# Earlier row loads, pool sums by thirds and DMA transposes in a streaming encoder layer on eight cores

## The reference

```
xn = rmsnorm(x); u, B, C, h = split(xn @ w_in)            # 4 x 512 columns
pool: per group of 128 channels, window w = 2, 4, 8, 16:
      mean of u over the last w rows - u, times w_pool[g], scaled
conv: B * (causal width-3 convolution of C * h)
x += rmsnorm(concat(group_rmsnorm(pool), group_rmsnorm(conv)) @ w_out)
x += rmsnorm(cross_attention(rmsnorm(x), memory keys and values))
x += rmsnorm(square(relu(rmsnorm(x) @ w_up)) @ w_down)
```

## Time and profile before

| what | us |
|---|---|
| median of 3 runs | 898.96 (898.18 to 900.38) |
| profiled execution, its own time | 901.45 |
| its span (core 1, the slowest) | 900.1 |
| spans of the eight cores | 893.8 to 900.1 |
| TensorE busy on core 1 | 859.5 (95%) |
| DVE busy, ACT busy | 448.9 (50%), 432.4 (48%) |

### The profile page before, as it was taken

How to read it: one execution, slowest core, us unless ns; L and a number is a source line. 1 busy time by engine, 2 the same in 40 slices (tenths; PEclk the granted TensorE clock), 3 DMA queues, 4 the chain that set the end, 5 groups by cost and what they waited for, 6 DMA issues and landing times.

```text
span 900.1 us, 14693 instructions; the slowest of 8 cores (893.8 to 900.1 us)
## 1 busy us (share of the span) xinstructions
PE 859.5 (95%) x5018; PEld 453.0 (50%) x5018; DVE 448.9 (50%) x772; ACT 432.4 (48%) x1043; POOL 53.0 (6%) x66
## 2 busy tenths in 40 slices
PE   7898898999999999999999998999899999999996
PEld 4565444664456666544444443457454444444442
DVE  3788687476872222232142877886684222200133
ACT  4557888466873333332132386886684333200122
POOL 1100100000000000000001000000000000000000
PEclk9989989999999999999999999999999999999998
DMA  9997376719585654636829992171716746426022
GB/s 195 194 155 110 76 118 105 127 28 206 76 151 81 98 80 62 102 88 115 117 100 120 236 228 82 40 96 23 95 21 110 107 69 94 59 36 87 8 94 94
DMA packets 66793, 91.89 MB, mean 102 GB/s; under 512 B 2936, under 2 KB 58360, under 8 KB 66208
## 3 DMA queue, kind: packets, MB, share of 16 engines
q0 software_dynamic: 58080, 60.95, 48.1%
q1 hardware_dynamic: 8640, 30.00, 10.2%
HBM read 137.49 MB, written 12.30 MB: 166 GB/s over the span
## 4 chain that ended last, share of the span: by engine, by line
PE 80%; ACT 9%; issue 4%; DVE 4%; DMA 2%; ACTq 0%; DVEq 0%; SPq 0%; POOLq 0%
PE psum L393 77%; PE psum L397 3%; ACT stg L411 3%; ACT xsb L411 3%; ACT st L411 2%; ACT un L411 2%; DMA ring<-w_in 1%; DMA X<-xp 1%; DVE un L423 1%; DVE xT L414 1%; DMA conv_p<-stg 1%; DVE X L423 0%; DVE un L414 0%; DVE un L418 0%; DVE xsb L418 0%
## 5 line engine op out<-in xcount | busy, mean ns | idle before, releaser
L393 PE MATMUL psum<-xT,ring 128*128 128x352 bf16 (+6 forms) x2336 | 413.0, 333 | 3.6 <-DVE xT L414 2.5
L393 PEld LDWEIGHTS psum<-xT,ring 128*128 128x128 bf16 x2336 | 226.5, 98 | 167.5 <-issue 6.6
L393 PE MATMUL psum<-ring,un 128*128 128x512 bf16 (+1 forms) x1408 | 302.6, 380 | 0.0
L411 ACT ACTIVATE un<-psum 128x352 bf16<-128x352 f32 (+9 forms) x258 | 125.0, 492 | 201.2 <-PE psum L393 198.9
L393 PEld LDWEIGHTS psum<-ring,un 128*128 128x128 bf16 (+1 forms) x1408 | 130.7, 98 | 157.7 <-issue 9.1
L414 DVE TENSOR_TENSOR un<-un 128x352 bf16<-128x352 bf16 (+5 forms) x176 | 84.8, 483 | 156.8 <-ACT un L411 156.8
L414 DVE TENSOR_TENSOR stg<-psum,gp 128x1024 f32<-128x1024 f32 (+3 forms) x51 | 53.1, 1042 | 106.6 <-ACT stg L411 57.6
L411 ACT ACTIVATE stg<-psum 128x1024 bf16<-128x1024 f32 (+3 forms) x51 | 44.5, 873 | 104.8 <-PE psum L393 102.6
L414 DVE TENSOR_TENSOR xT<-psum,gcs 128x1024 bf16<-128x1024 bf16 (+2 forms) x52 | 60.0, 1155 | 35.7 <-PE psum L397 35.2
L393 PE MATMUL psum<-ring,mg 128*128 128x512 bf16 (+1 forms) x320 | 75.8, 388 | 0.0
L423 DVE SCALAR_TENSOR_TENSOR X<-stg,st,X 128x1024 f32<-128x1024 f32 (+3 forms) x51 | 56.3, 1104 | 6.8 <-DVE stg L414 4.7
(11 more groups left out here) (95 smaller groups left out, 517.1 us busy)
## 6 DMA issues: line engine op xcount, KB each, us to landing
ring<-w_up POOLq DMA_DIRECT2D x16, 1024.0 KB, 14.2
ring<-w_down POOLq DMA_DIRECT2D x16, 1024.0 KB, 10.7
X<-xp SPq DMA_DIRECT2D x16, 512.0 KB, 14.0
yp<-X SPq DMA_DIRECT2D x16, 512.0 KB, 2.7
ring<-w_in POOLq DMA_DIRECT2D x7, 1024.0 KB, 11.4
ring<-w_out POOLq DMA_DIRECT2D x4, 1024.0 KB, 31.8
ring<-w_q POOLq DMA_DIRECT2D x4, 1024.0 KB, 22.7
stg<-xp SPq DMA_DIRECT2D x8, 512.0 KB, 4.3
```

The costliest lines, as they stand in the source:

```text
L393: P.add("pe", lambda e: e.matmul(out, lhsT=lhsT, rhs=rhs, start=start, stop=stop), reads=[lhsT, rhs], writes=[out])
L411: P.add("act", lambda e: e.activation(out=out, in_=in_, func=func, scale=scale, **kw), reads=rd, writes=wr)
```

## The change

- SP's queue loses the identity and the gain columns (`idf`, `gcs`), which ACT's queue asks for now. Block 2's load (L1181) waits for block 1 to have landed, not for w_in.
- The chain that makes blocks ready is written anew. Block 2 (number 3) is prepared wholly ahead of the first projection; block 3 (number 4) behind the second unit; fewer fillers. It uses five bf16 slots in another place, for which the pool scratch `SW` shrinks.
- Pool sums go in three tiles of columns (272, 512 and 288 with the running streams) and the first enters at unit 4 of phase 0, among the preparation of blocks 4 to 7.
- Mappings of the first tile begin at (1, 3) and not (1, 8); those of the last end at (3, 1) and not (3, 4).
- The evacuations of u that DVE does are units 4 to 7 and not 5, 7, 9, 11. The adds that fill `psel` go to the end of phase 3.
- In `hook0`, the 8 TensorE transposes per block of group 1 become one DMA transpose on SP's queue, and the gain is multiplied in place 7 units later.

```diff
--- before.py
+++ after.py
@@ -281,9 +281,9 @@
 
 U_TILES = [[(0, 272), (272, 528), (528, 784), (784, 1072)], [(16, 528), (528, 1040)]]
 A_TILES = [[(14, 368), (368, 720), (720, 1072)], [(16, 528), (528, 1040)]]
-P_TILES = [[(0, 528), (528, 1072)], [(16, 528), (528, 1040)]]
-P_AT = [(12, 16), (4, 8)]
-MAP_AT = [[[(1, 8), (1, 9), (1, 10), (1, 11)], [(2, 3), (2, 5), (2, 7), (2, 9)], [(2, 11), (3, 0), (3, 2), (3, 4)]],
+P_TILES = [[(0, 272), (272, 784), (784, 1072)], [(16, 528), (528, 1040)]]
+P_AT = [(4, 12, 16), (4, 8)]
+MAP_AT = [[[(1, 3), (1, 5), (1, 7), (1, 9)], [(1, 11), (2, 1), (2, 3), (2, 5)], [(2, 7), (2, 9), (2, 11), (3, 1)]],
           [[(1, 4), (1, 5), (1, 6), (1, 7)], [(2, 2), (2, 3), (2, 4), (2, 5)]]]
 F_TILES = [[(16, 368), (368, 720), (720, 1072)], [(16, 528), (528, 1040)]]
 Q_TILES = [F_TILES[0], [(16, 400), (400, 784), (784, 1040)]]
@@ -593,7 +593,7 @@
     V_OFF = 4 * UW * 4
     P_OFF = V_OFF + 4 * VW * 4
     S_OFF = P_OFF + 4 * MW * 2
-    SW = [592, 528]
+    SW = [528, 528]
     sA_OFF = S_OFF
     sB_OFF = [sA_OFF + 16 * w for w in SW]
     SQ_OFF = [sB_OFF[g] + 12 * SW[g] for g in range(2)]
@@ -782,7 +782,7 @@
                     k = P_AT[grp].index(n_all)
                     poolq.extend((P_TILES[grp][k][0], f) for f in pool_ops(grp, *P_TILES[grp][k]))
                 if ph == 0:
-                    ev_u(jj, proj(w, jj, lo, hi), lo, hi, grp == 0 and n in (5, 7, 9, 11))
+                    ev_u(jj, proj(w, jj, lo, hi), lo, hi, grp == 0 and 4 <= n < 8)
                 elif ph == 1:
                     ev_C(jj, proj(w, jj, lo, hi), lo, hi)
                 elif ph == 2:
@@ -1168,17 +1168,17 @@
 
     halo = stg[0:16, 0:D]
     memx = [uf(PT_OFF + 8192, 1024), uf(PT_OFF + 12288, 1024)]
-    xs_pro = [ub(P_OFF + 2048 * i, 1024) for i in range(4)]
+    xs_pro = [ub(V_OFF + 2048 * i, 1024) for i in range(5)]
     xs_mem = [ub(KVP_OFF + 2048 * i, 1024) for i in range(2)]
     stT = mgf[0:32, 0:512]
     scT = mgf[0:4, 512:1024]
     dma("sp", halo, xh[:, :], rd=False)
     first = stream.load_first()
     dma("sp", Xs(0), xrow(0, 0), rd=False)
-    dma("sp", idf[:, :], ident[:, :], rd=False)
-    dma("sp", gcs[:, :], gcol[:, :], rd=False)
+    dma("act", idf[:, :], ident[:, :], rd=False)
+    dma("act", gcs[:, :], gcol[:, :], rd=False)
     dma("sp", Xs(1), xrow(0, 1), rd=False)
-    P.add("sp", lambda e: e.dma_start(out=Xs(2), in_=xrow(0, 2)), reads=[first], writes=[Xs(2)], dma=True)
+    P.add("sp", lambda e: e.dma_start(out=Xs(2), in_=xrow(0, 2)), reads=[Xs(1)], writes=[Xs(2)], dma=True)
     for b in (3, 4):
         dma("sp", Xs(b), xrow(0, b), rd=False)
     dma("sp", pvt[:, :], pvec[:, :], rd=False)
@@ -1192,7 +1192,7 @@
     stream.load(after=Xs(4))
     vmemset(epsb[:, :], EPS)
     vmemset(ones[:, :], 1.0)
-    vmemset(ub(S_OFF, 512), 1.0)
+    vmemset(ub(65536, 512), 1.0)
     vmemset(bd64[:, :], 0.0)
     vmemset(bd64[0:64, 0:64], 1.0)
     vmemset(bd64[64:128, 64:128], 1.0)
@@ -1201,14 +1201,10 @@
         dma("sp", stT[b * 16 + 1:b * 16 + 16, :], spool[b], rd=False)
     dma("sp", scT, sconv.rearrange("b r c -> (b r) c"), rd=False)
     vcopy(idb[:, :], idf[:, :])
-    tt(psel[:, 0:32], idf[:, 0:32], idf[:, 32:64], ALU.add)
-    tt(psel[:, 0:32], psel[:, 0:32], idf[:, 64:96], ALU.add)
-    tt(psel[:, 0:32], psel[:, 0:32], idf[:, 96:128], ALU.add)
-
     pre_q = [(halo, 16, 9, 0, xT3[:, :, 0:16])]
     for b in (0, 1, 2, 3, 4, 5, 6, 7, SMP):
         pre_q.append((Xs(b), rows(b), skey(b), 0, xT3[:, :, xcol(b):xcol(b) + rows(b)]))
-    pre_xs = [xs_pro[k % 4][0:q[1], :] for k, q in enumerate(pre_q)]
+    pre_xs = [xs_pro[k % 5][0:q[1], :] for k, q in enumerate(pre_q)]
 
     pre_tb = {}
 
@@ -1228,7 +1224,7 @@
         xap, r, key, gi, dst = pre_q[k]
         gain_out(pre_tb.pop(k), r, gi, dst)
 
-    warm = ub(S_OFF, 512)
+    warm = ub(65536, 512)
 
     def c_w(n):
         out = bank()
@@ -1239,9 +1235,9 @@
         for w in text.split():
             {"A": c_a, "S": c_s, "T": c_t, "G": c_g, "W": c_w}[w[0]](int(w[1:]))
 
-    CHAIN = {0: "A3", 2: "A4", 3: "W8 S3 T3 G3 W8 S4 T4 G4 A5 A6 W4", 4: "A7", 5: "S5 T5 S6 G5 A8", 6: "T6 G6", 7: "S7 A9",
-             8: "T7 S8 G7", 9: "T8 G8", 10: "S9", 11: "W3 T9 G9 W2"}
-    chain("W11 A0 A1 S0 T0 G0 W2 A2 S1 T1 G1 W7 S2 T2 G2 W5")
+    CHAIN = {0: "A4", 1: "S4 T4 G4", 2: "A5", 3: "A6", 4: "A7", 6: "S5 W2 T5", 7: "S6 W3 G5 T6 W3 G6 A8",
+             8: "S7 T7 A9", 9: "G7 S8", 10: "T8 G8 S9", 11: "W2 T9 G9 W2"}
+    chain("W11 A0 A1 S0 T0 G0 W2 A2 S1 T1 S2 G1 W3 T2 G2 A3 W6 S3 T3 G3")
 
     def states_in():
         tb = tbank()[0]
@@ -1258,6 +1254,10 @@
                 states_in()
             elif n == 15:
                 tt(psg[:, :], pvt[:, 0:4], pvt[:, 16:20], ALU.mult)
+        elif phase == 3 and n == 11:
+            tt(psel[:, 0:32], idf[:, 0:32], idf[:, 32:64], ALU.add)
+            tt(psel[:, 0:32], psel[:, 0:32], idf[:, 64:96], ALU.add)
+            tt(psel[:, 0:32], psel[:, 0:32], idf[:, 96:128], ALU.add)
         elif phase == 2 and n == 0:
             load_gp("g_mix_post")
 
@@ -1287,7 +1287,9 @@
             xs = pre_a(sl, 128, 12 + j % 2)
             if j + 2 < NB:
                 dma("sp", sl, xrow(1, j + 2), rd=False)
-            later(2, lambda: pre_b(xs, 128, 0, xT3[:, :, xcol(j):xcol(j) + 128]))
+            dst = xT3[:, :, xcol(j):xcol(j) + 128]
+            P.add("sp", lambda e: e.dma_start(out=dst, in_=xs, transpose=True), reads=[xs], writes=[dst], dma=True)
+            later(7, lambda: tt(dst, dst, gcs[:, 0:8].unsqueeze(2).to_broadcast([128, 8, 128]), ALU.mult))
 
     def cache_loads():
         for mc in range(2):
```

## The result

The changed kernel takes **905.45 us** (4 executions, 905.04 to 905.64) against 898.57 of the kernel before beside it on the chip: ratio 1.0073, 95% interval 1.0056 to 1.0091. It is slower by 6.9 us, where 2.8 less was forecast, and lies above the range. The profiled execution's own time is 905.28; its slowest core is 7.

A forecast was written before the change was run, and what follows sets the result against it. TensorE was taken to wait for VectorE in phase 0 and VectorE and ScalarE in phase 3, and to be bound by its own work under w_down; 5.0 - 4.2 - 3.6 = -2.8, from 898.96 to 896.2 us, range 891 to 903.

The forecast's parts named there:

- Step 1: First loads: block 2 lands at 16, w_in at 18.5, so the first projection starts at about 19.7, 3.2 us later.
- Step 2: Block 3's preparation behind the first projection's units: second tile starts at 26.2, 1.0 us earlier than 27.2.
- Clock: I take no change: Granted clock was 1.00 in both stalling windows of the kernel before; forecast to stay so.
- Step 3: VectorE's list until phase 0's fourth tile, with pool steps of 6.4: that tile starts at 45.7 against 40.7, +5.0 us.
- Step 4: Phase 3: two of three mappings leave ScalarE's list there, so of TensorE's 6.3 us idle 2.1 stay, -4.2.
- Step 5: Group 0's w_down: eight sets of TensorE transposes go, -3.6 us; DMA transposes taking 4 us, hidden up to 10.
- C: Rival: phase 0's cost is not given back, phase 3 gives only 1.0; +2.4, 901.4 us; chance 0.22.
- D: Rival: DMA transposes beyond 10 to 12 us under w_down stall VectorE, then TensorE; 909.7 us at 16; chance 0.15.

The follow-up runs named there:

- the last run: The kernel before with DMA transposes, sorted last waits, and the second and third tiles' mappings moved up out of phase 3: 891.72 us, ratio 0.9923.

## Why the prediction was wrong, point by point

The forecast was a sum of three terms, +5.0, -4.2 and -3.6. Measured on the median core they are +10.8, -3.3 and -3.8, with -0.7 between w_out and w_down, and +1.2 from group 1's stage A to the end, in which the stretch behind the last matmul is +1.5: +4.2 for the median core. The faults lie in the first term above all, in the second, and in what the sum left out.

- **Step 1, "3.2 later".** The landings were near: block 2 at 17.8 (16 forecast), w_in's second half at 5.0 + 14.4 = 19.4 (18.5), the first projection at 20.3 on the median core (19.7). But the difference was taken from core 1 with its 16.5, which stands 1.3 behind the median core of before (15.25). So it is +5.0 and not 3.2. This did no harm to the sum, which goes by 45.7 against 40.7, and there core 1 is only 0.3 off. Still, the first projection before starts at 14.2 to 16.5 by core, so its reference has to be the median of the cores.
- **Step 2, "the second tile starts at 26.2", and "Clock: I take no change".** This is the step that failed first. The second tile starts at 27.33 + 1.93 = 29.3 on core 7 and at 28.8 on the median core, so 1.9 later than the 26.9 of before and not 1.0 earlier. The prediction gave the first units 0.97 each; they took 1.9, behind a TensorE that had waited for 4.76 with fewer fillers in between. The clock of 1.00 in the windows of before was taken over for a stretch in which TensorE would be busy for less of the time. The run with more fillers had 1.00 again and took 3.0 off.
- **Step 3, "+5.0 until the fourth tile".** Its prices were right: VectorE's work from the first pool add to the last G comes to 16.1 (51.34 - 31.33 less 3.9 of waits) against 16.3. Its start was 31.3 (30.7 on the median core) and not 27.6, which is what the step before handed on, and its waits 3.9 and not 1.8; these two errors make the 5.5 by which the fourth tile missed 45.7. S of block 4 is recorded behind pool steps, so TensorE's transposes are late, run at the lower clock, and VectorE waits for them in turn. One engine's delay was counted, and the other's answer to it not. That the pool steps' cover is gone was right, and the runs show it directly: 4.0 at unit 4, nothing at units 12 and 13. But they are less than half of the 10.8, and the step called them the heart of it.
- **Step 4, "phase 3 -4.2".** Phases 1 to 3 gave 3.3, but phase 3 only 2.7 of it; 0.9 came in phase 1, where none was forecast (the pool tiles alone give it too: 15.7 for 16.7), and 0.3 was lost in phase 2. TensorE's idle time in phase 3 was to fall from 6.3 to 2.1. It fell to 3.9, and on five cores the clock is below 1.00 there as well. The wait that remains was foreseen as about 2; on core 7 it is 2.79 and 1.09, with units at the lower clock behind (clock 0.86 in that window). It goes with the one mapping left: in the last run, which has none in phase 3, that phase takes 19.9. So the mechanism was right and the term too large. The reason given for phases 1 and 2, that TensorE shows no wait there, holds only with the new pool tiles: with the old ones the mappings cost 4.4 in phase 1. Such a missing wait doesn't say that a bank would be free in time.
- **Step 5, "-3.6".** Right: 3.8, and 3.6 alone. The transpose takes 7.7 and not 4, up to 10.6, and the bound of 10 to 12 up to which it is hidden held: VectorE waited for 12.0 us in three gains, ScalarE for 14.8, and TensorE for none. The Trainium skill, VectorE: DVE Perf Modes, The three transpose paths, has 1309 ns for one 128x128 through DMA, an estimate of 10.5 for eight in a row; the trace, with 4.7 to 10.6, agrees with it as an upper end. The Trainium skill, DMA: Bandwidth & Descriptors, has 261 GB/s for DMA transposes in its section Latency and other measured facts (the prediction names the section Bandwidth), an estimate of 1 us; the trace doesn't agree with that.
- **What no step had.** The end of the program (+1.5), because the edit of one stage was followed only within it, although its eight DMAs more shift the semaphores that SP's queue takes in turn to the end of the program. And the slowest core: 1.7 above the median core before, 3.4 after. This goes with the early load of block 2: in the four kernels that have it the slowest core stands 2.8 to 3.4 above the median one, in the ten others 1.6 to 2.5, and among these in the changed kernel with that load alone put back 1.9. With the load put back the median core is 2.3 slower than the changed kernel's, the time only 0.9. The load thus seems to help the median core and hardly the time; with 4 to 12 executions of a kernel and 2.5 beside 2.8 this isn't shown beyond doubt, and what would make the load differ from core to core was not tried.
- **The rivals.** C had the cost of phase 0 kept and was nearest with 901.4; but its reason, a phase 3 that gives only 1.0, isn't what happened. D's wait, at 0.15, didn't come. The chance of 0.06 for a phase 0 not given back that ends beyond 2.7 was too low: the errors of steps 2 and 3 have the same sign, and the second followed from the first.

## What to carry to other kernels

Where TensorE waits for another engine, count the wait, then the work behind it at the lower clock, then what that makes late on the first engine; fillers taken away from such a place cost even if they computed nothing. An engine's extra work is free or not by its place in that engine's list, which one run with the same steps a few units later tells. And before an edit's parts are judged together, run each alone: here one part (the transposes) gained and another (mappings) gained in a gentler place, and both were hidden by a start that cost more than they gave.

## What the runs showed of the hardware that was not expected

- The granted clock, at 1.00 in the earlier trace rows, was 0.69 in a window in which TensorE was busy for 3.35 of 8 us. Behind a wait of 4.76 there, sixteen matmuls of 272 columns took 3.83 for 1.93, and in the run of the mappings alone, behind a wait of 3.55, eight of 352 columns took 2.55 for 1.35 at a granted clock of 0.51, so 1.2 for 2.4 GHz; matmuls without use in the waits brought the first window back to 1.00.
- A DMA transpose of a 128x1024 block, from one on-chip buffer to another, lands after 4.7 to 10.6 us beside weight loads, and its issue keeps SyncE for 1.2 to 5.4 us.
- The order in which this kernel's SyncE waits for its last DMAs at the end of the program is worth 1.5 us.
